# Gate projection of a hybrid mLSTM / sliding-window layer: low parts of the gate weights placed behind the high parts in one stationary tile

## What is computed

```python
mq, mk, mv, mo, mi, mf, sq, sk, sv = split_in_proj(x @ w_in)
...
i_pre = softcap(mi.astype(f32) + b_ig).transpose(0, 2, 1)
f_pre = softcap(mf.astype(f32) + b_fg).transpose(0, 2, 1)
h, C, n, m = mlstm_chunkwise(q, k, v, i_pre, f_pre, *ml_state)
```

## Time and profile before

| | us |
|---|---|
| median of 3 runs | 2487.85 |
| lowest, highest | 2483.61, 2489.39 |
| profiled execution | 2485.81 |
| its span, first to last instruction | 2484.0 |
| PE busy | 2447.8 |
| DVE, ACT, POOL busy | 989.6, 941.8, 1296.5 |
| mean granted TensorE clock | 0.992 |

### The profile page before, as it was taken

How to read it: one execution, slowest core, us unless ns; L and a number is a source line. 1 busy time by engine, 2 the same in 40 slices (tenths; PEclk the granted TensorE clock), 3 DMA queues, 4 the chain that set the end, 5 groups by cost and what they waited for, 6 DMA issues and landing times.

```text
span 2484.0 us, 33074 instructions
## 1 busy us (share of the span) xinstructions
PE 2447.8 (99%) x13451; PEld 2367.1 (95%) x13451; DVE 989.6 (40%) x1630; ACT 941.8 (38%) x1433; POOL 1296.5 (52%) x548
## 2 busy tenths in 40 slices
PE   8999999999999899999999999999999999999997
PEld 7999999999999789999999999999999999999997
DVE  4455564645656561323351123522325213351103
ACT  3335454545555333222433233432234223342222
POOL 4455454444545345555555555455555555555553
PEclk9999999999999889999999999999999999999999
DMA  5444444343467745343334433344333443343332
GB/s 196 148 113 133 139 121 135 102 144 105 123 188 228 250 125 185 112 145 125 113 106 142 147 127 111 103 145 147 122 107 111 146 146 122 107 138 119 120 122 74
DMA packets 141437, 335.19 MB, mean 135 GB/s; under 512 B 13694, under 2 KB 78806, under 8 KB 140630
## 3 DMA queue, kind: packets, MB, share of 16 engines
q1 hardware_dynamic: 141286, 333.08, 42.9%
HBM read 304.92 MB, written 29.13 MB: 134 GB/s over the span
## 4 chain that ended last, share of the span: by engine, by line
PE 96%; DVE 2%; DMA 1%; SPq 1%; issue 1%; ACT 0%; ACTq 0%; DVEq 0%
PE acc L1712 10%; PE acc L1710 10%; PE acc L1711 10%; PE acc L268 9%; PE acc L270 9%; PE acc L269 9%; PE kd L1712 5%; PE fb L1712 5%; PE kd L1710 5%; PE fb L1710 5%; PE kd L1711 5%; PE fb L1711 5%; PE fb L620 1%; PE w L597 1%; PE w L610 1%; DMA raw<-in_wB 1%
## 5 line engine op out<-in xcount | busy, mean ns | idle before, releaser
L1634 POOL TENSOR_TENSOR l_wlo<-l_raw,l_whi 128x1024 fp32r<-128x1024 f32 (+1 forms) x297 | 822.3, 2769 | 675.7 <-ACT l_whi L1648 675.7
L1648 ACT ACTIVATE l_whi<-l_raw 128x1024 fp32r<-128x1024 f32 (+1 forms) x297 | 340.6, 1147 | 1008.2 <-PE acc L1712 478.7
L255 POOL TENSOR_TENSOR wlo<-raw,whi 128x1024 fp32r<-128x1024 f32 x150 | 371.0, 2476 | 470.0 <-ACT whi L249 470.0
L268 PE MATMUL acc<-xh,whi 128*128 128x416 f32 x1200 | 433.2, 361 | 0.0
L270 PE MATMUL acc<-xh,wlo 128*128 128x416 f32 x1200 | 425.7, 355 | 0.0
L269 PE MATMUL acc<-xl,whi 128*128 128x416 f32 x1200 | 422.7, 352 | 0.0
L249 ACT ACTIVATE whi<-raw 128x1024 fp32r<-128x1024 f32 x150 | 158.5, 1057 | 403.3 <-PE acc L270 297.7
L1710 PE MATMUL acc<-xh,l_whi 128*128 128x416 f32 x880 | 310.8, 353 | 0.0
L1712 PE MATMUL acc<-xh,l_wlo 128*128 128x416 f32 x880 | 310.6, 353 | 0.0
L1711 PE MATMUL acc<-xl,l_whi 128*128 128x416 f32 x880 | 307.2, 349 | 0.0
L268 PEld LDWEIGHTS acc<-xh,whi 128*128 128x128 f32 x1200 | 228.0, 190 | 8.4 <-issue 6.5
(11 more groups left out here) (350 smaller groups left out, 4246.1 us busy)
## 6 DMA issues: line engine op xcount, KB each, us to landing
l_raw<-in_wB SPq DMA_DIRECT2D x220, 512.0 KB, 3.5
raw<-in_wA SPq DMA_DIRECT2D x110, 512.0 KB, 3.6
l_raw<-in_w SPq DMA_DIRECT2D x80, 704.0 KB, 4.0
raw<-in_wB SPq DMA_DIRECT2D x40, 512.0 KB, 4.0
xraw<-in_xT SPq DMA_DIRECT2D x32, 416.0 KB, 5.6
stage<-in_xT SPq DMA_DIRECT2D x40, 208.0 KB, 4.1
pre<-stage SPq DMA_DIRECT2D x40, 208.0 KB, 3.9
xs_b<-xsT SPq DMA_DIRECT2D x16, 512.0 KB, 8.5
```

The costliest lines, as they stand in the source:

```text
L255: self.nc.gpsimd.tensor_tensor(self.wlo[:, n % 4], self.raw[:, n % 4], self.whi[:, n % 3].bitcast(F32), ALU.subtract).then_inc(self.lo_don ...
L268: pe.matmul(bank[:, 0:TG], hi[:, a], self.xh[x][:, a], start=(a == 0), stop=False)
L1634: nc.gpsimd.tensor_tensor(wlo[:, n % 4, 0:k], raw[:, n % 4, 0:k], whi[:, n % 3, 0:k].bitcast(F32), ALU.subtract).then_inc(S["lo_done"], 1)
L1648: nc.scalar.activation(whi[:, n % 3, 0:k], raw[:, n % 4, 0:k], ACT.Copy).then_inc(S["hi_done"], 1)
```

## The change

The high part of the gate weights stays in columns 0 to 7 of the tile, and the low part moves to columns 8 to 15 of the same tile, `gw`. One pass with high x and one with low x then give 16 rows: 0 to 7 with high weights, 8 to 15 with low ones. All 16 are evacuated, stored, and loaded again (13 loads for nine), and VectorE adds low rows to high rows in four instructions before it scales the biases. The product of low weight and low x, left out before, is now part of the sum. One memset of GpSimd falls away. The step counters move up by four.

```diff
@@ load_gates
-        get(t[n][:], bass.AP(tensor=io["gateT"].tensor, offset=i * H * NT, ap=[[NT, H], [C, NC], [1, C]]))
-        get(t[n + "_s"][:], io["gateT"][i * H:i * H + H, SEQ:NT])
+        for part, row in (("", i * H), ("_low", 2 * H + i * H)):
+            get(t[n + part][:], bass.AP(tensor=io["gateT"].tensor, offset=row * NT, ap=[[NT, H], [C, NC], [1, C]]))
+            get(t[n + part + "_s"][:], io["gateT"][row:row + H, SEQ:NT])
@@ class Stream
+    def gate_product(self, pe, acc, k, w, v):
+
+        bank, x = acc[k % 2], VISITS[v][1]
+        if k >= 2:
+            pe.wait_ge(self.acc_free, k - 1)
+        for a in range(KD):
+            if a % XQ == 0:
+                pe.wait_ge(self.x_split, 4 * v + a // XQ + 1)
+            pe.matmul(bank[:, 0:TG], w[:, a], self.xh[x][:, a], start=(a == 0), stop=False)
+            last = pe.matmul(bank[:, 0:TG], w[:, a], self.xl[x][:, a], start=False, stop=(a == KD - 1))
+        last.then_inc(self.acc_full, 1)
@@ tiles
-    ghi = early.sb("ghi", [P, KD, P], F32R)
-    glo = early.sb("glo", [P, KD, P], F32R)
-    grow = early.sb("grow", [8, 2, TG])
+    gw = early.sb("gw", [P, KD, P], F32R)
+    grow = early.sb("grow", [16, 2, TG])
@@ GpSimd
-        nc.gpsimd.memset(ghi[:].bitcast(F32), 0.0).then_inc(g_zero, 1)
-        nc.gpsimd.memset(glo[:].bitcast(F32), 0.0).then_inc(g_zero, 1)
+        nc.gpsimd.memset(gw[:].bitcast(F32), 0.0).then_inc(g_zero, 1)
         pool.wait_ge(g_hi, 1)
-        pool.wait_ge(g_zero, 2)
-        nc.gpsimd.tensor_tensor(glo[:, :, 0:8], graw[:], ghi[:, :, 0:8].bitcast(F32), ALU.subtract).then_inc(g_split, 1)
+        nc.gpsimd.tensor_tensor(gw[:, :, 8:16], graw[:], gw[:, :, 0:8].bitcast(F32), ALU.subtract).then_inc(g_split, 1)
@@ TensorE
-                x.product(pe, acc, gate_tile(i), ghi, glo, i, True)
+                x.gate_product(pe, acc, gate_tile(i), gw, i)
@@ ScalarE
-        act.wait_ge(g_zero, 2)
-        nc.scalar.activation(ghi[:, :, 0:8], graw[:], ACT.Copy).then_inc(g_hi, 1)
+        act.wait_ge(g_zero, 1)
+        nc.scalar.activation(gw[:, :, 0:8], graw[:], ACT.Copy).then_inc(g_hi, 1)
@@ VectorE
-            nc.vector.tensor_copy(grow[:, i % 2], acc[k % 2][0:8, 0:TG]).then_inc(acc_free, 1)
+            nc.vector.tensor_copy(grow[:, i % 2], acc[k % 2][0:16, 0:TG]).then_inc(acc_free, 1)
...
-                dve.wait_ge(g_loaded, 16 * 9)
+                dve.wait_ge(g_loaded, 16 * 13)
+                for name, low in (("gi", "gi_low"), ("gf", "gf_low"), ("gi_s", "gi_low_s"), ("gf_s", "gf_low_s")):
+                    d(nc.vector.tensor_tensor(g[name][:], g[name][:], g[low][:], ALU.add))
```

More of the change, by code:

```diff
@@ L347, in mixers @@
         ("gi", [R, C]), ("gf", [R, C]), ("gi_s", [H, NS]), ("gf_s", [H, NS]),
+        ("gi_low", [R, C]), ("gf_low", [R, C]), ("gi_low_s", [H, NS]), ("gf_low_s", [H, NS]),
         ("small", [R, 4]), ("small_s", [H, 4]), ("m0_sb", [H, DB]))}
@@ L414, in mixers @@
     dve_s = m.sem("c_dve")
-    CAPPED_BIAS, ONE_MORE, OWN, BEFORE, MAXIMA, EXPONENTS, U, SAMPLE_X, COLS = 2, 4, 10, 15, 17, 19, 20, 37, 41
+    CAPPED_BIAS, ONE_MORE, OWN, BEFORE, MAXIMA, EXPONENTS, U, SAMPLE_X, COLS = 6, 8, 14, 19, 21, 23, 24, 41, 45
     SROWS, BIASES, SIGMOIDS, LOGS, SCALES = 1, 5, 11, 13, 17
@@ L1818, in bass_hymba_step @@
 def bass_hymba_step(nc, io):
-    io["gateT"] = nc.dram_tensor("gateT", [8, NT], F32, kind="Internal").ap()
+    io["gateT"] = nc.dram_tensor("gateT", [16, NT], F32, kind="Internal").ap()
     io["xsT"] = nc.dram_tensor("xsT", [H, 2, NT], F32, kind="Internal").ap()
```

## The result

| | kernel before | changed kernel |
|---|---|---|
| median of 20 runs each, us | 2485.48 | 2488.87 |
| lowest, highest, us | 2482.36, 2489.39 | 2485.88, 2493.53 |
| profiled execution, us (its span) | 2485.81 (2484.0) | 2489.2 (2487.4) |
| mean granted TensorE clock | 0.992 | 0.991 |

The ratio of the runs is 1.0014, with a 95% interval from 1.0008 to 1.002: the change makes the kernel 3.4 us slower. The two profiled executions lie just as far apart, 3.4 us. The forecast was 2486.0, about 0.7 us less than I took the kernel before to be. The sign was wrong, and the measured time is 2.9 us above the forecast.

A forecast was written before the change was run, and what follows sets the result against it. TensorE, busy 99% of the span, was taken as the bound. Matmuls saved -6.8 us, PE's longer wait +4.4 and low clock +1.6 sum to -0.8 us; against an average of 2486.7 that gave 2486.0 us, range 2479.5 to 2489.5.

The forecast's parts named there:

- What was taken off PE: Gate products 0 to 4: fewer matmuls save 0.75 us in product 0 and 6.0 in the others, sum 6.8 us.
- The cascade, steps 1 to 7: Slabs 12 to 17: more gate loads delay a weight load; adds and scans wait for POOL, costing PE 4.4 + 1.6 us.
- steps 6 and 7: Before L693: scans held by POOL make PE wait 4.4 us more; the low clock behind it loses 1.6 us.
- rival A: Gate recurrence: adds find POOL idle or scalings catch up, nothing reaches L693; -6.8 us, 2479.9 us, chance 0.22.
- The step that failed: From slab 18 on, and the wait before L702: all is timed from its slab's end and moves along unchanged.
- in time by 0.2 us: Gate product 3: the last quarter's split ends at 74.16, wanted at 74.39, so PE does not wait.
- B: Gate recurrence: scans run beside POOL or one step fits a gap; -4.6 us, 2482.1 us, chance 0.16.
- C: After the wait before L693: low clock lasts over 5.2 us; with 10 us it is +2.2, 2488.9 us, chance 0.08.
- D: Gate products: 16 matmuls last as long as 24 because of x's arrival; only losses stand, +6, 2492.7 us, chance 0.01.
- the 0.05 for slower: Whole kernel: chance 0.05 of being slower by over 0.2%, made of late x, a long low clock and scatter.

The follow-up runs named there:

- e6: The changed kernel unaltered, profiled once more; 2486.51 us in one run, no ratio given.
- e3: Changed kernel with the weight load of slab 16 issued between the two halves of the gate loads, after seven of thirteen; 2483.47 us, ratio 0.999.
- e1: Kernel before with `gateT` declared with 16 rows, of which 8 are used; 2488.89 us, ratio 1.0008.
- e5: Kernel before with `xsT` declared twice as long, so it stays and the tensors behind it move; 2486.35 us, ratio 0.9998.
- e13: Changed kernel with its 16-row `gateT` declared last and 8 rows of unused room left ahead of `xsT`; 2484.54 us, ratio 0.9997.
- e16: Kernel before with only its 8-row `gateT` declared last, so `xsT` lies 66,560 bytes lower; 2494.16 us, ratio 1.0038.
- e2: Changed kernel with the low rows stored into a DRAM tensor of their own, declared last; 2487.09 us, ratio 1.0002.
- e4: Kernel before with the low part in columns 32 to 39 of one tile, summed when the bank is emptied, eight rows stored; 2485.34 us, ratio 0.9995.
- e10: Kernel before with the second quarter's split of x for gate products 2 to 4 one slab earlier; 2486.65 us, ratio 1.0004.
- e11: Changed kernel with the second quarter's split of x for gate products 2 to 4 one slab earlier; 2487.85 us, ratio 1.0007.
- e12: Changed kernel with only its 16-row `gateT` declared last, so `xsT` lies 66,560 bytes lower; 2495.53 us, ratio 1.0043.

## Why the prediction was wrong

**What was taken off PE: nearly right.** 6.8 us were forecast and 6.2 were there when slab 12 started (5.8 in e6). Read product by product, the 0.6 lies in two places. Product 0 saved 0.5 us and not 0.75: its restart came at 14.38 for 14.28, and slab 1 started at 22.18 where 21.98 was reckoned, its bank emptied at 22.03. Product 3 lasted 71.97 - 68.64 = 3.33 us and not 3.0, and saved 1.2 of 1.5. Products 1, 2 and 4 saved their 1.5 each.

**The cascade, steps 1 to 7: right in mechanism and near in size.** The weight load late by 2.2 us, adds of over 2 us in POOL's shadow, both scans held, PE's wait for `own` 4.12 us (forecast 4.4), low pitch for 2.8 us behind it (forecast 3.5). At 127 us the sum of the forecast was -0.8 and the trace shows -0.6; e3 took the cascade away and gained 6 us, the price of steps 6 and 7. Of the adds, the second and third were held and not the first and second: the first passed, as rival A's case has it, and the end was the same.

**The step that failed** is the sentence behind the sum: "What lies behind (n = 18 and on, the wait before L702) is timed from the end of its slab and moves along unchanged." It holds from 127 to 800 us and fails at 820, where one broadcast load takes 6.2 us for 3.9 and the wait behind it grows by 3.7 us: -0.4 + 3.7 = 3.3, and the span is 3.4 us longer. I had taken the change as an edit of instructions and went through each queue for what moves past what. The one line of it that resizes a DRAM tensor I priced at nothing, without looking at what is declared behind it. e1 and e5 show that this line lengthens the wait with no instruction changed. Its price is 3.3 us in the average waits of all profiles, and 4 us between the medians of the changed kernel and e13; e1's median is 2 us up, with an interval that reaches to nothing. A loss of this size turns the forecast gain of 0.7 us into the measured loss.

**A second step was wrong, in the profile by a little and in the runs by more:** "in time by 0.2 us" at the splits of product 3. The sum moved the splits along with the product. In the changed kernel the product starts 3.49 us sooner than before and the three splits 3.12, so they end 2.40 us behind its start in place of 2.03. Timelines of DVE and PE:

```profile
66.62 4.42 DVE L296 TENSOR_TENSOR xl<-xraw,xh 128x832 fp32r<-128x832 f32 x3 [1.73 <-ACT xh L245]
...
71.10 0.46 PE L283 MATMUL acc<-xh,gw 128*128 128x416 f32 x1
```

They end at 71.04, and the last quarter was due at 68.64 + 2.26 = 70.90. It starts at 71.10, the quarter before it was 0.02 us late, and these two hitches cost the 0.3 us above, in the changed kernel, in e6 and in e3 alike. In the other five of eight such profiles the third split ran into the next `wlo`, and the wait was about 2.1 us. A margin of 0.2 us read from one execution is no margin where the order of two engines at a lock hangs on it.

**The rivals.** A and B fell with the held adds and scans. C, the only one on the slower side, had the right sign by the wrong mechanism: the low stretch lasted 2.8 us and not over 5.2. D fell with 3.02 us for product 1. The true cause was none of the four, and nothing in the 0.05 for slower stood for work far from the edit. That the time lies within the stated 2479.5 to 2489.5 us is luck: the upper part of that range was there for C. The base was also high: I averaged four executions to 2486.7, and 20 runs gave 2485.48.

## What to carry to other kernels

A change that resizes or adds a DRAM tensor can move all that is declared behind it: name each load that reads there many times over in small pieces, and compare its landing before and after, before any story of schedule. Where a cut is to shorten an engine's work, look for every release that stands within a microsecond of being late; here three things (a load behind small loads, a split behind two others, a placement) cost about 2 to 6 us each, beside a gain of 6, and only the kernels with all three mended kept it to the end. Where a kernel has the same instructions and another median, as e16, look at the addresses. Two single profiles are not enough for that: those of the kernel before are 3.4 us apart with nothing changed.

## What I had not expected of the hardware

- The landing of a broadcast load depends on where its source is declared to lie, at steps of 66,560 bytes: 3.6 to 4.3, 5.6 to 6.7 or 4.1 us for 128 copies of 8 rows of 128 bytes, and 8.5 to 9.0 or 11.5 to 11.7 us for 128 copies of 8 rows of 512. Which place is good for the one is not good for the other. 66,560 is 260 x 256, so a row starts as far from a multiple of 256 bytes as before. The Trainium skill (DMA: Bandwidth & Descriptors, "How a descriptor splits into AXI transactions") counts the transactions of a descriptor from its size and from whether it starts on a multiple of 256 bytes. By that the three places would be alike, and the runs show otherwise. What in the address decides was not tried.
- A slow load in the queue shows on the issuing side: SP's issue of `s_n`, six DMAs behind `s_xs`, took 4.32 us in place of 1.01 (3.2 to 5.3 in the five profiles with `xsT` higher, 0.6 to 1.7 in the eleven at the old place), and `s_kc`, a load from elsewhere, landed in 7.5 us in place of 4.5.
- `tensor_tensor_scan` with two inputs in SBUF is held by an operation of POOL like a `tensor_tensor`: 2.48 and 2.38 us, and 0.42 when POOL was idle.
- The same wait of 1.94 us before L702 or its counterpart was followed by a stretch of 6 to 10 matmuls at the low pitch in e2, e4, e5, e10, e11, e12, e13 and e16, and by none in the kernel before, the changed kernel and the other eight profiles. It costs 1 to 1.6 us when it comes. Behind 840 us between some 22 and 43 matmuls are at the low pitch, in one and the same kernel too, which is worth up to 3.3 us. Both are part of the scatter of these runs.
